# A decoder's attention stage: a new slot order on every engine, six value pages in the ring, probabilities transposed into the score banks

## What is computed

```python
# prompt group, 512 tokens, in blocks of 128 queries
sc = einsum('bqhd,bkhd->bhqk', qi, k) * scale + ci[..., :, None] - c_k[:, :, None, :]
sc = where(causal, sc, NEG_INF)
o  = einsum('bhqk,bkhd->bqhd', softmax(sc), v)
...
# sample group: 8 requests, 16 pages of 128 cached keys and values each
k_past = k_pool[page_table];  v_past = v_pool[page_table];  r_past = reverse_cumsum(logf_past)
s_past = einsum('bqhd,bkhd->bhqk', q, k_past) * scale + cq[..., :, None] + r_past
s_new  = einsum('bqhd,bkhd->bhqk', q, k) * scale + cq[..., :, None] - cq[:, :, None, :]   # causal
p = softmax(concatenate([s_past, s_new]))
o = einsum(p[:p_len], v_past) + einsum(p[p_len:], v)
```

## Time and profile before

| | us |
|---|---|
| median of 3 runs | 2018.95 |
| lowest and highest run | 2005.68, 2023.38 |
| profiled execution, its own time | 2022.65 |
| its span in the trace | 2020.9 |
| TensorE busy in the span | 1770.0 |
| VectorE, ScalarE, GpSimd busy | 942.3, 561.5, 111.4 |

### The profile page before, as it was taken

The page is one execution under the profiler, slowest core; times in us unless marked ns, Lnnn a source line. Parts: engine busy times, 40 slices in busy tenths (PEclk is TensorE's granted clock), DMA queues, the critical chain, the costliest instruction groups (busy, mean ns, idle before and its releaser), DMA issues.

```text
span 2020.9 us, 37879 instructions
## 1 busy us (share of the span) xinstructions
PE 1770.0 (88%) x15111; PEld 1542.6 (76%) x15111; DVE 942.3 (47%) x1367; ACT 561.5 (28%) x1008; POOL 111.4 (6%) x217
## 2 busy tenths in 40 slices
PE   5999565979999999899977687788779899999999
PEld 4876443979999999889954444444439799999998
DVE  5388776453333322467546755555523533333221
ACT  3210223232222211243332333433322322222211
POOL 1000000000000000144310000000000000000000
PEclk9999876999999999999977788888879899999999
DMA  3211031212222322223343677777772222222331
GB/s 118 60 46 32 21 100 42 82 54 83 83 83 80 88 87 86 66 68 79 80 149 98 220 237 246 270 252 254 248 245 69 62 83 83 83 82 82 95 101 53
DMA packets 240211, 224.87 MB, mean 111 GB/s; under 512 B 12290, under 2 KB 200340, under 8 KB 240090
## 3 DMA queue, kind: packets, MB, share of 16 engines
q1 hardware_dynamic: 229776, 201.13, 31.8%
q0 software_dynamic: 8896, 18.79, 3.1%
q10 hardware_dynamic: 1418, 3.29, 0.5%
HBM read 215.37 MB, written 7.80 MB: 110 GB/s over the span
## 4 chain that ended last, share of the span: by engine, by line
PE 76%; DVE 12%; DMA 4%; issue 3%; ACT 3%; SPq 2%; ACTq 0%; DVEq 0%; POOL 0%; POOLq 0%
PE ps L1490 56%; PE ps L1920 4%; DMA vring<-in_cache_fox_v_dram 4%; PE ps L1696 3%; PE ps L1965 2%; PE ps L1899 1%; DVE tmp L440 1%; PE ps L1472 1%; DVE yc L719 1%; SPq L2078 1%; DVE aL L444 1%; DVE rb L435 1%; DVE rb L450 1%; PE ps L1558 1%; PE ps L1881 1%
## 5 line engine op out<-in xcount | busy, mean ns | idle before, releaser
L1490 PE MATMUL ps<-aH,wH 128*128 128x288 f32 x2224 | 488.5, 302 | 49.1 <-DVE aL L444 33.5
L1490 PE MATMUL ps<-aL,wH 128*128 128x288 f32 x2224 | 481.4, 298 | 0.0
L1490 PE MATMUL ps<-aH,wL 128*128 128x288 f32 x2224 | 481.0, 298 | 0.0
L1490 PEld LDWEIGHTS ps<-aH,wH 128*128 128x128 f32 x2224 | 362.7, 191 | 58.0 <-issue 35.6
L421 DVE TENSOR_TENSOR wL<-raw,wH 128x1024 fp32r<-128x1024 f32 (+1 forms) x179 | 232.0, 1296 | 331.9 <-ACT wH L1046 328.8
L1490 PEld LDWEIGHTS ps<-aL,wH 128*128 128x128 f32 x2224 | 363.5, 191 | 0.0
L1490 PEld LDWEIGHTS ps<-aH,wL 128*128 128x128 f32 x2224 | 363.3, 191 | 0.0
L1046 ACT ACTIVATE wH<-raw 128x1024 fp32r<-128x1024 f32 (+1 forms) x179 | 198.9, 1111 | 381.4 <-PE ps L1490 352.2
L1490 PE MATMUL ps<-gH,wH 128*128 128x288 f32 x704 | 151.6, 296 | 0.0
L1490 PE MATMUL ps<-gH,wL 128*128 128x288 f32 x704 | 151.1, 295 | 0.0
L1490 PE MATMUL ps<-gL,wH 128*128 128x288 f32 x704 | 151.0, 295 | 0.0
(11 more groups left out here) (307 smaller groups left out, 1802.3 us busy)
## 6 DMA issues: line engine op xcount, KB each, us to landing
kset<-in_cache_fox_k_dram SPq DMA_DIRECT2D x128, 384.0 KB, 4.3
vring<-in_cache_fox_v_dram SPq DMA_DIRECT2D x128, 384.0 KB, 4.8
raw<-in_w_gate_up_dram SPq DMA_DIRECT2D x88, 512.0 KB, 3.8
raw<-in_w_down_dram SPq DMA_DIRECT2D x32, 704.0 KB, 4.6
raw<-in_fox_w_in_dram SPq DMA_DIRECT2D x21, 512.0 KB, 3.9
raw<-in_w_out_dram SPq DMA_DIRECT2D x16, 512.0 KB, 4.2
raw<-in_conv_w_in_dram SPq DMA_DIRECT2D x14, 512.0 KB, 3.8
raw<-in_w_mem_kv_dram SPq DMA_DIRECT2D x8, 512.0 KB, 3.7
```

Of the source, the lines that this page charges most:

```text
L1490: mm = nc.tensor.matmul(ps[:, 2 * slot + h, 0:HT], weights[:, w], a[:, k0 + k, h * HT:(h + 1) * HT], start=(first and k == 0 and weights i ...
```

## The change

Four things change in the merged stage, and nothing else in the kernel but the ScalarE copies that filled `qr`.

The ring of value pages has six places in place of four (the room comes from `qr`, which is gone). SyncE's list has the key chunks of a slot later by one, so that their score set lies at least a slot back, and the value pages reach two further ahead.

The order in a slot is another one on each engine. TensorE has the score set and two pages first, then the transpose of the step's probabilities, then the other two pages, `sample_probT`, and pv last but for the next scores. The high and low parts of a step's product are taken one slot later (`step_hi(s-2)`, `step_lo(s-2)`), ScalarE copies the transposed probabilities behind the next step's exponential, and the second forget row of a pair is made five slots apart from the first one's place, in the middle of its slot.

`sample_probT` no longer takes turns at banks 6 and 7: the seventeen blocks go to the score banks 0 to 3, and ScalarE copies them with three instructions. The next batch's first score set therefore waits for these copies (`pt_taken`).

`spread` reads the queries where they lie, with sixteen copies of 32 partitions in place of four of 128.

```diff
-    VRING = 4
+    VRING = 6
...
+        TURNS += [("probT", s - 1)] if step else []
         if cc == 1 and b >= 2:
             TURNS += [("out", b - 2)]
+        if s % 5 == 0 and s < STEPS:
+            TURNS += [("ncb", s // 5, 1)]
         TURNS += [("pv", s - 1)] if step else []
-        if cc == 3 and s < SLOTS:
-            TURNS += [("PT", b, g) for g in range(4)]
...
                 if s < STEPS:
                     step_sums(s)
+                if 2 <= s <= STEPS + 1:
+                    step_lo(s - 2)
                 if cc == 2 and b < NB:
                     sample_new(b)
...
-                if 1 <= s <= STEPS:
-                    step_lo(s - 1)
...
-                for m in range(4):
-                    nc.scalar.activation(qx4[:].rearrange("p (j m c) n -> p j m c n", m=4, c=2)[:, :, m, :, NQ * m:NQ * m + NQ],
-                                         qr[:].rearrange("p (j m) c n -> p j m c n", m=4)[:, :, m, :, NQ * b:NQ * b + NQ], ACT.Copy)
+                for e in range(2):
+                    for c in range(2):
+                        for a in range(4):
+                            rows = slice(DH * e + DQ * c, DH * e + DQ * c + DQ)
...
+                            nc.scalar.activation(mine, qkT[rows, 0:HP, SEQ + NQ * b:SEQ + NQ * b + NQ].rearrange("p (j m) q -> p j m q", m=2), ACT.Copy)
...
-                for g in range(4):
-                    n = min(5, NP - 5 * g)
-                    bank = turn_bank(("PT", b, g))
-                    wait_turn(act, ("PT", b, g))
...
+                act.wait_ge(pt_ready, b + 1)
+                nc.scalar.activation(pTs[:, 0:15, :].rearrange("p (g k) r -> p g (k r)", g=3), ps[:, 0:3, 0:5 * ROWS], ACT.Copy)
+                nc.scalar.activation(pTs[:, 15, :], ps[:, 3, 0:ROWS], ACT.Copy)
+                nc.scalar.activation(pTs[0:NS, NP, :], ps[0:NS, 3, ROWS:2 * ROWS], ACT.Copy).then_inc(pt_taken, 1)
...
-                if 1 <= s <= STEPS:
-                    step_probT(s - 1)
                 if cc == 0 and b >= 2:
                     sample_scale(b - 2)
+                if 2 <= s <= STEPS + 1:
+                    step_hi(s - 2)
                 if cc == 3 and b < NB:
                     sample_exp(b)
                 if s < STEPS:
                     step_exp(s)
+                if 1 <= s <= STEPS:
+                    step_probT(s - 1)
...
                     if b:
-                        pe.wait_ge(sexp_done, b)
+                        pe.wait_ge(pt_taken, b)
...
-            for s in range(SLOTS + SPB - 1):
-                for n in (2 * s + NCH, 2 * s + NCH + 1):
-                    if n < NB * NCH:
+            for s in range(1, SLOTS + SPB):
+                for n in (2 * s + NCH - 2, 2 * s + NCH - 1):
+                    if NCH <= n < NB * NCH:
                         key_chunk(n)
...
-                for n in range(4 * (s - 3), 4 * (s - 2)):
-                    if n >= VRING:
+                for n in range(4 * (s - 4) + VRING, 4 * (s - 3) + VRING):
+                    if VRING <= n < NB * NP:
                         value_page(n)
```

More of the change, by code:

```diff
@@ L124, in fox_step @@
         return k, e, [(n, hp + n, t, col, keys) for n, t, col, keys in parts]
-    TURNS = [("ncb", 0, 0), ("ncb", 0, 1)]
+    TURNS = [("ncb", 0, 0)]
     for s in range(SLOTS + SPB):
@@ L130, in build @@
         step = 1 <= s <= STEPS
-        TURNS += [("probT", s - 1)] if step else []
         if cc == 2 and s < SLOTS:
             TURNS += [("new", b)]
+        TURNS += [("probT", s - 1)] if step else []
         if cc == 1 and b >= 2:
             TURNS += [("out", b - 2)]
+        if s % 5 == 0 and s < STEPS:
+            TURNS += [("ncb", s // 5, 1)]
         TURNS += [("pv", s - 1)] if step else []
-        if cc == 3 and s < SLOTS:
-            TURNS += [("PT", b, g) for g in range(4)]
         if (s + 1) % 5 == 0 and s + 1 < STEPS:
-            TURNS += [("ncb", (s + 1) // 5, e) for e in range(2)]
+            TURNS += [("ncb", (s + 1) // 5, 0)]
     TURNS += [("out", NB - 1)]
@@ L941, in step_top @@
                 pr = prob[:, i % 2, :]
-                if k == 0:
-                    for n in range(2):
-                        wait_taken(dve, ("ncb", i // 5, n))
+                if k < 2:
+                    wait_taken(dve, ("ncb", i // 5, k))
                 dve.wait_ge(f_scores, i + 1)
@@ L1333, in _, with c_keys @@
             sample_memory(1, u + len(MEM_UNITS))
[L1335 to L1339, removed]
+            def c_keys(two, n):
+                wait_turn(act, ("ncb", two, n))
+                nc.scalar.activation(ncb[:, n, :], turn_bank(("ncb", two, n)), ACT.Copy).then_inc(taken(("ncb", two, n)), 1)
             def spread(b):
@@ L1865, in turn, with c_keys @@
                 return turn_bank(key)
[L1867 to L1872, removed]
+            def c_keys(two, n):
+                bank = turn(("ncb", two, n))
+                h = 2 * (two - two % 2 + n) + two % 2
+                nc.tensor.matmul(bank, ident[0:DH, h:h + 1].broadcast_to([DH, P]), ncT[0:DH, :], start=True, stop=True).then_inc(turn_ready, 1)
             def step_scores(i):
@@ L1944, in sample_probT @@
                 pe.wait_ge(sexp_done, b + 1)
[L1945 to L1953, removed]
+                for k in range(NP):
+                    nc.tensor.transpose(ps[:, k // 5, k % 5 * ROWS:(k % 5 + 1) * ROWS], S[:, k * P:(k + 1) * P], ident[0:ROWS, 0:ROWS])
+                nc.tensor.transpose(ps[0:NS, 3, ROWS:2 * ROWS], S[:, NPAST:NPAST + NS], ident[0:ROWS, 0:ROWS]).then_inc(pt_ready, 1)
             def values(b, k):
@@ L1988, in _ @@
                 step = 1 <= s <= STEPS
-                if step:
-                    step_probT(s - 1)
+                first = NP * cc // SPB
+                last = NP * (cc + 1) // SPB
                 if s < SLOTS and cc % 2 == 0:
@@ L1995, in _ @@
                 if b:
-                    values(b - 1, 4 * cc)
-                    values(b - 1, 4 * cc + 1)
+                    for k in range(first, first + 2):
+                        values(b - 1, k)
+                if step:
+                    step_probT(s - 1)
                 if cc == 1 and b >= 2:
                     sample_out(b - 2)
+                if s % 5 == 0 and s < STEPS:
+                    c_keys(s // 5, 1)
+                if b:
+                    for k in range(first + 2, last):
+                        values(b - 1, k)
+                if cc == 3 and s < SLOTS:
+                    sample_probT(b)
                 if step:
                     step_values(s - 1)
[L2002 to L2006, removed]
                 if (s + 1) % 5 == 0 and s + 1 < STEPS:
-                    c_keys((s + 1) // 5)
+                    c_keys((s + 1) // 5, 0)
                 if s + 1 < STEPS:
```

33 lines of the change are left out of this document (10 added, 23 removed).

## The result

| | us | against the kernel before, 95% interval |
|---|---|---|
| before, median of 20 runs | 2018.70 | |
| changed kernel, median of 20 runs | 2033.44 (2022.76 to 2050.94) | 1.0071 [1.0054, 1.0088] |
| predicted | 2008 | 0.995 |
| profiled execution: own time, span | 2050.94, 2049.0 | |

The change costs 0.7% where 0.6% of gain was forecast: inside the range, within the 1% named there, and on the wrong side. That it lies inside is luck: the upper end of the range was set for pages that stay late, and they came in time.

What follows compares the result with a forecast made beforehand. Late value pages, issued late by SyncE's queue, were taken to bound the merged stage. D -27.6, A +11.9, B +3, forget rows +8, edges -2 -2 -2.6 sum to -11.3 us: 2008 us (-0.6%), 80% range 1975 to 2036.

Steps and rivals of the forecast that it cites:

- pages that stay late: Rival in the merged stage: value pages still come late, D keeps its wait, 2038 us; chance 0.10.
- the price of a copy: ScalarE's spread before the next batch's set: sixteen copies at 0.135 us from start to start, 2.2 us.
- the forget rows: Second product mid-slot in slots 5, 10, 15, 20, 25: slot 15 +6, slots 5 and 25 about +1 each; sum +8.
- The rival's condition: Rival that ScalarE's batch-boundary chain ends slower, deciding from 0.236 us a spread copy; 2052 us, chance 0.13.
- the A slots: Slots of cc 0 (4, 8, ... 28): set waits 2.4 us where 0.9, +1.7 each, seven times +11.9.
- C: Slots of cc 2: probT only changes places, the gap and slow stretch stay; 0.
- D: Slots of cc 3: page wait goes, sample 12.8 to 8.0 us; six give -27.6, -23.0 without slot 15's forget row.
- B: Slots of cc 1: output transpose waits for its bank, idle 4.3 us against 2.90; +0.5 each, six times +3.0.
- Edges: Stage's ends: first batch -2, last batch -2, tail pages -2.6 at some 1.3 us a page; -6.1 in the table.
- the signs named for being wrong: Merged stage: D page waits 2 us or more, aL chain under 5, spread above 4, clock above 0.92 or below 0.8.

Runs made afterwards that it cites:

- e15: Changed kernel with all sixteen spread copies reading and writing within the first 32 partitions, so sample scores differ; 2018.01 us, 0.9987.
- e13: Changed kernel with the sixteen copies' loops turned round, destination partition group outermost, same work; 2035.46 us, 1.0077.
- e4: Changed kernel with a ring of four value pages in place of six, same order of issues; 2044.25 us, 1.0115.
- e6: Changed kernel with the ring of four, and with qr and the four-copy spread back; 2017.34 us, 0.9983.
- e10: Changed kernel with the low part ahead of the key transposes only in slots 5, 10, 15, 20, 25 and 30; 2023.01 us, 1.0000.
- the two moves: Changed kernel with low part ahead of key transposes (2002.55 us), with spread's sixteen copies moved into slot cc 2 (2017.76 us), with both (1969.72 us).
- e9: Changed kernel with twenty more matmuls of 8 columns on TensorE ahead of the merged stage; one time, 2031.26 us.

## Why the prediction was wrong

Two terms of the sum failed: the price of a copy in `spread`, which alone makes the difference between no change and a loss, and the forget rows.

**The price of a copy.** The step was "0.135 from start to start by their mean of 0.235". The mean was right (0.239 in the changed kernel), the distance was not: it came from a row of four copies of 128 partitions that overlap, and the sixteen do not, (3.99 - 0.24) / 15 = 0.25. The row that I named as the dearest was the nearest in kind, sixteen copies of 32 partitions from `qkT` to other partitions, and showed it: 0.53 each in the earlier trace rows, as long as one lasts. I read it as a price for 384 columns. The estimate of 0.227 us from the Trainium skill ("VectorE: DVE Perf Modes", section "The TRN2 errata — SBUF-src ops pay a fixed extra latency per instruction") was nearer than my row, and the trace is 10% above it. The rival's condition, 0.236 us a copy, was met, without the 0.53 that its 2052 was worked out with.

e15 is the test of that step: with the copies at 2.21 us, the 2.2 of the prediction, the A slots are longer than before by 10.7 us where 11.9 were predicted (24.4 as it was), and the kernel runs at 0.9987 [0.9967, 1.0007]: 17 of the 25 us between forecast and result, some of them in C, which falls by 5.5 us from e13 to e15. So the working of A was right for its price. e15's products have other inputs, since `qx4` is filled otherwise; e4 and e6, whose products have the changed kernel's, point the same way: 27 us for 3.35 us a spread.

**Forget rows.** This term was +8; in e13 the slots 5, 25 and 15 took 11.8 us more than that (8.4 - 2.5 + 7.3 - 1.4). I counted slot 15's push-back at upper-clock durations, and took slots 5 and 25 for B slots that wait anyway; slot 5 has no output transpose: it waited 2.5 us for a page before, now waits 5.3 for the bank, and the forget row's own product takes 2.07 us behind that wait. e10 gives 14 us back from these slots.

**D** was right: 8 us in the sample (1419.1 to 1427.1 in slot 23), -23.9 in e13 for -23.0. The 1.83 us of the earlier trace rows that stood for its chain ended with L1003, the sample output's low part, which comes behind the chain. **B** was right in its wait (4.3 to 4.6) and a little better in sum. **C** was taken as unchanged; +3.1 in e13, more in the slowest run, whose gaps inside the `cc` 2 sets are 16.3 us against 11.1 before and 11.7 in e13 by the rows marked issue. **Edges**: -2.9 and not -6.1; that `spread(0)` with its sixteen copies stands ahead of the first set was left out (slot 0 takes 13.2 us in e4 and 9.6 with the four copies of e6). The 1.3 us for a page of the tail is in no row: 22.9 / 16 is 1.4. Of the signs named for being wrong, two showed: spread takes 4.67 us (3.99 + 0.68), and the stage's clock is 0.79 (0.81 in e13).

## What to carry to other kernels

Take a copy's price from start to start only from a row that also agrees in whether source or destination partitions change from one copy to the next; where none does, work out the sum with a copy's own duration as well (0.24 us here, against 0.25 from start to start). Before moving a step behind another on an engine, look who waits for its last instruction: here one instruction of 0.4 us, put ahead of 3.4 us of transposes, was worth 31 us. And a gain in front of a chain that ends elsewhere counts only together with that chain: the two moves gave 50 us singly and 64 together.

## What the runs showed of the hardware

ScalarE's copies of 48 columns on 32 partitions last 0.22 to 0.24 us each whatever their place, but start 0.13 us apart within one group of 32 partitions ((2.21 - 0.23) / 15) and 0.24 to 0.25 apart where source or destination goes to another group. The Trainium skill ("ScalarE: Activation LUTs", section "What ACT_TABLE_LOAD costs") says that instructions back to back overlap by about 93 ns and gives 186 ns plus 0.833 a column, an estimate of 0.133 us from start to start here: e15 agrees, and in e13 nothing overlaps.

In the changed kernel's stage TensorE stood still eight times within a set, for 0.7 to 3.3 us, and each time went on 1.35 to 1.54 us after a 16 KB packet of the instruction queue had ended; 40 such packets fall in the stage, so most held nothing up. The place moves with the program's length (e9, in one slot). The Trainium skill ("Runtime: NRT & Kernel Launch", section "Instruction fetch mechanics") names blocks of that size and calls the crossing of one mostly hidden; that fits the other packets, and in these sets it was not hidden.
